# A streaming encoder layer with gathered experts: four groups of tiles instead of five, the sample's tokens on 128 partitions, the bias expanded from DRAM

## The chip, the cores and the metric

The kernel runs on one core of a Trainium2 chip. All times are device microseconds (us) of that core; lower is better. The time of a kernel is the median of its runs. One execution was profiled, and all rows of the trace are of that one.

## The reference

One layer for 1024 prompt tokens and 64 sample tokens (which have a cache of 512 keys and a running state), model width 1024, all in 32-bit floats:

```
xn = rmsnorm(x);  z = xn @ w_in                        # 1024 x 5632: q k v | f i q g | gate_a gate_b
o_a = softmax(q k' / 8 + bias[clipped distance]) v     # 8 heads of 64, own chunk of 64 and 8 before
o_b = HGRN2 recurrence in chunks of 64                 # 4 heads, state 128 x 128, rmsnorm, swish gate
h = x + (sigmoid(gate_a) * (o_a @ w_a) + sigmoid(gate_b) * (o_b @ w_b)) @ w_out
q = rmsnorm(h) @ w_query                               # 8 heads x 2 halves of 128
s = q . sub_keys; top 16 of each half, top 16 of the 256 sums  -> idx, gate (softmax)
y = rmsnorm(h + sum over 8 heads x 16 of gate * gelu(xn . u[idx]) * v[idx])    # 16384 experts
```

Outputs are y of both, the new keys and values (512 prompt rows and the 64 of the sample) and the new states. Each token of each head fetches 16 rows of u and 16 of v, 4 KB each.

## The kernel before

**Tiles and groups.** Tokens are cut into nine tiles: 0 to 7 are 128 prompt tokens each, and the tile SAMPLE has 64. `GROUPS` (line 37) lists which tiles are mixed together and at which column of the group's activations each begins: SAMPLE and 0 (192 wide), 1 and 2, 3 and 4, 5 and 6 (256 wide each), and 7 (128 wide). All tile-order loops follow this list, so SAMPLE comes first.

**Mixing, stages A to I of a group** (`mix(g)` on each engine). A: load x to `hx`, norm, turn to `xnT`. B: q, k, v. C: attention, one step for each head and tile, on keys of up to five tiles (`keys_of`, 646); SAMPLE's are the four of the cache, turned in group 0 (627), and its own. D: gate_a and w_a. E: projections of HGRN2. F: HGRN2, tile after tile. G: gate_b and w_b. H: w_out, second norm. I: w_query and, for each tile and head, scores against the sub-keys and top-k (VectorE, 1470 to 1526). "fm" products (574) have a 128 x 128 piece of the weights stationary and the group's W columns moving; "tm" products (578) have a tile's tokens stationary and 256 columns of weights moving. `plan_projections` cuts the weights into 38 blocks of 1 MB for a group; each group loads all 38 again through `wring`, three blocks deep, on SP's queue. TensorE records two instructions for each matmul of 32-bit floats.

**Experts.** A "head" q is one expert head of one tile: 72 in all. GpSimd issues 16 indirect gathers of u rows and, two heads later, 16 of v rows (`rows_in`, 547 to 560), one row of 4 KB for each token's partition, into `ring` of R = 13 slots of 128 x 1024. A slot is free again when its reader is done: VectorE reads every u row (dot product with x, line 1549) and the even v rows (1559); TensorE reads the odd v rows through a diagonal matrix of weights (854), made by ScalarE (1170). For SAMPLE all of these work on 64 partitions. At a new tile GpSimd waits for `h_out`, loads `xt` and `acc` (538 to 545), and waits for each head's top-k (`tk_done`, 553).

**Order of the work.** `interleave` (120) writes the order out for every engine alike: first the mixing of group 0 alone up to its first top-k (the start-up); then the expert heads of group g as units, with the slices of the rest of group g's top-k and of `mix(g + 1)` up to its first top-k spread between them by the estimated costs of `slices`. In the last group, where only top-k slices are left, a factor of 2.5 packs them into the first 40% of the units.

**Start-up.** SP's queue (412 to 430) loads small vectors, `rel` (the bias values in reverse), the sub-keys and the state, then x; writes `rel_scr` (427) from 8 partitions, every partition's line of 767 values repeated 128 times, shifted by one, 640 values each; then `sk_scr` (430), the turned sub-keys; then loads weights (436). ScalarE begins stage B only when `sk_scr` has landed (928). Bias tiles are loaded from `rel_scr` for each head (475) while attention runs, and VectorE adds them (1297). Engines wait for each other between stages by `enter` and `leave`.

## Time and profile before

| what | value |
|---|---|
| median of 3 runs | 4497.34 us (4483.53 to 4503.79) |
| the profiled execution's own time | 4459.93 us |
| its span, first to last instruction | 4458.2 us |
| TensorE clock granted, mean of the span | 0.806 of 2.4 GHz |
| moved by DMA | 1408.39 MB, 316 GB/s |
| gathers | 1152 of u rows, 1152 of v rows |
| loads of weight blocks | 190 of 1024 KB |

The span is what the trace covers; the time of the execution is 1.7 us longer, and the median of the runs is 37.4 us above it. PE is TensorE's matmuls, PEld its weight loads, DVE VectorE, ACT ScalarE, POOL GpSimd, SP the queue of loads and stores.

### The profile page before, as it was taken

What the parts mean: (1) busy time and instruction counts of PE and PEld (TensorE: products, weight loads), DVE (VectorE), ACT (ScalarE), POOL (GpSimd) and SP (SyncE); (2) the same over time, 40 slices, a digit from 0 to 9 for tenths busy, and PEclk for the clock granted to TensorE, in tenths of its full rate; (3) what the DMA queues carried; (4) which work ended last, traced back from release to release, by engine and by line L of the source; (5) the groups of instructions that cost most, each with busy time, mean ns of one, the idle gap of its engine ahead of it and who ended that gap; (6) DMA issues with size and microseconds to landing.
All of it is one profiled execution on the core that took longest, in us unless ns stands there. A gap on an engine that the chain in (4) does not pass through costs nothing. (4 is left out here: it accounts for less than half of the span.)

```text
span 4458.2 us, 36425 instructions
## 1 busy us (share of the span) xinstructions
PE 3141.0 (70%) x11064; PEld 1982.6 (44%) x11064; DVE 3094.0 (69%) x6491; ACT 843.8 (19%) x2079; POOL 2651.6 (59%) x2349
## 2 busy tenths in 40 slices
PE   3968558997777468876875588868765667666556
PEld 3847314464454235653652265636532345343212
DVE  0142996648849986579579956595699764858975
ACT  1221112222111123122111222211111121111101
POOL 0000566647747676568456766585577765766776
PEclk9778658598898678987987698988887788788777
DMA  5415758999999899999999999999999999999999
GB/s 130 128 59 168 179 158 198 236 287 343 355 345 356 318 340 343 396 348 346 355 346 333 332 330 385 358 349 364 334 393 346 372 374 380 359 384 372 369 404 363
DMA packets 531664, 1408.39 MB, mean 316 GB/s; under 512 B 47952, under 2 KB 223568, under 8 KB 530704
## 3 DMA queue, kind: packets, MB, share of 16 engines
q0 software_dynamic: 317856, 1149.91, 71.4%
q1 hardware_dynamic: 211088, 246.98, 17.2%
q10 hardware_dynamic: 2528, 9.18, 0.6%
q8 instruction: 91, 1.49, 0.1%
q14 instruction: 101, 0.83, 0.1%
HBM read 1385.98 MB, written 19.92 MB: 315 GB/s over the span
## 5 line engine op out<-in xcount | busy, mean ns | idle before, releaser
L854 PE MATMUL PS<-ring,diag 128*128 128x512 f32 (+1 forms) x2304 | 1481.5, 783 | 828.9 <-DMA ring<-in_peer_v,idx 590.0
L558 POOL DMA_INDIRECT ring<-in_peer_u,idx x1152 | 1347.0, 1169 | 730.1 <-issue 313.2
L558 POOL DMA_INDIRECT ring<-in_peer_v,idx x1152 | 1286.4, 1117 | 632.5 <-DVE hid L1549 316.0
L1549 DVE CUSTOM_DVE_ANT_0 ring<-ring,xt 128x1024 f32<-128x1024 f32 (+1 forms) x1152 | 1396.7, 1220 | 357.3 <-DMA ring<-in_peer_u,idx 218.5
L854 PEld LDWEIGHTS PS<-ring,diag 128*128 128x128 f32 (+1 forms) x2304 | 488.1, 230 | 1541.2 <-issue 1197.7
L574 PE MATMUL PS<-xnT,wring 128*128 128x256 f32 (+2 forms) x3840 | 781.4, 365 | 164.8 <-DMA wring<-in_w_in 94.8
L574 PEld LDWEIGHTS PS<-xnT,wring 128*128 128x128 f32 x3840 | 695.7, 204 | 287.7 <-issue 156.8
L1559 DVE SCALAR_TENSOR_TENSOR acc<-ring,wk,acc 128x1024 f32<-128x1024 f32 (+1 forms) x576 | 739.5, 1284 | 62.0 <-DMA ring<-in_peer_v,idx 49.0
L544 POOL DMA_DIRECT2D xt<-xn_scr x9 | 5.4, 602 | 423.9 <-DMA xn_scr<-arena 423.9
L1170 ACT ACTIVATE diag<-ident,wk 128x128 f32<-128x128 f32 (+1 forms) x576 | 203.3, 387 | 229.1 <-PE PS L854 135.4
L578 PE MATMUL PS<-wring,xnT 128*128 128x256 f32 (+1 forms) x864 | 201.7, 392 | 21.9 <-DMA wring<-in_w_in 21.8
L578 PEld LDWEIGHTS PS<-wring,xnT 128*128 128x128 f32 (+1 forms) x864 | 162.7, 190 | 66.3 <-DMA wring<-in_w_in 27.2
L1297 DVE SCALAR_TENSOR_TENSOR arena<-PS,bias 128x640 f32<-128x640 f32 (+3 forms) x72 | 47.9, 665 | 190.3 <-DMA bias<-rel_scr 90.3
L578 PE MATMUL PS<-wring,arena 128*128 128x256 f32 (+1 forms) x576 | 143.4, 410 | 41.1 <-DVE arena L1445 34.3
L578 PEld LDWEIGHTS PS<-wring,arena 128*128 128x128 f32 (+1 forms) x576 | 114.7, 201 | 74.4 <-issue 49.3
L574 PE MATMUL PS<-arena,wring 128*128 128x256 f32 (+2 forms) x640 | 126.5, 352 | 3.9 <-DMA wring<-in_w_branch_b 2.5
L1141 ACT ACTIVATE arena<-PS 128x256 f32<-128x256 f32 (+1 forms) x72 | 27.6, 383 | 521.5 <-PE PS L822 353.1
L574 PEld LDWEIGHTS PS<-arena,wring 128*128 128x128 f32 x640 | 110.1, 192 | 27.2 <-issue 11.3
L1242 DVE TENSOR_TENSOR arena<-PS,arena 128x256 f32<-128x256 f32 (+2 forms) x40 | 15.3, 383 | 147.0 <-PE PS L574 146.9
L1155 ACT ACTIVATE arena<-arena 128x16 f32<-128x16 f32 (+1 forms) x72 | 22.2, 308 | 495.8 <-DVE arena L1506 495.5
L662 PEld LDWEIGHTS PS<-kT,arena 64*128 64x128 f32 (+1 forms) x560 | 83.3, 214 | 44.4 <-issue 35.6
L662 PE MATMUL PS<-kT,arena 64*128 64x128 f32 (+2 forms) x560 | 99.2, 328 | 3.9 <-ACT mark_a L865 2.6
(170 smaller groups left out, 2686.6 us busy)
## 6 DMA issues: line engine op xcount, KB each, us to landing
wring<-in_w_in SPq DMA_DIRECT2D x110, 1024.0 KB, 16.4
wring<-in_peer_query SPq DMA_DIRECT2D x40, 1024.0 KB, 11.7
wring<-in_w_out SPq DMA_DIRECT2D x20, 1024.0 KB, 10.3
ring<-in_peer_u,idx POOLq DMA_INDIRECT x1152, 7.1
ring<-in_peer_v,idx POOLq DMA_INDIRECT x1152, 7.0
bias<-rel_scr SPq DMA_DIRECT2D x80, 144.0 KB, 6.1
wring<-in_w_branch_a SPq DMA_DIRECT2D x10, 1024.0 KB, 23.8
wring<-in_w_branch_b SPq DMA_DIRECT2D x10, 1024.0 KB, 14.7
```

Of the source, the lines that this page charges most:

```text
L558: pool.indirect_dma_start(ring[0:tile_rows[tn], n % R, :], None, u_tab if kind == "u" else v_tab, bass.IndirectOffsetOnAxis(ap=idx[0:tile_ ...
L574: mm = pe.matmul(PS[:, n % 2, 0:W], w[:, k, s * P:(s + 1) * P], act_in[:, k, 0:W], start=(k == 0), stop=(k == nk - 1))
L578: mm = pe.matmul(PS[0:rows, n % 2, 0:ncol], act_in[:, k, c0:c0 + rows], w[:, k, :], start=(k == 0), stop=(k == nk - 1))
L662: mm = pe.matmul(PS[0:rows, bank + n // 4, (n % 4) * P:(n % 4) * P + nk], q, kk[p0:p0 + 64, h // 2, 0:nk], start=True, stop=True)
L854: mm = pe.matmul(PS[0:rows, 6 + half, :], diag[0:rows, seq % ND, 0:rows], ring[0:rows, n % R, 512 * half:512 * (half + 1)], start=(h == 0 ...
L1141: act.activation(s1[0:rows, o % 2], PS[0:rows, 2 + o % 2, 0:2 * P] .rearrange("p (a b) -> p a b", a=2), ACT.Copy).then_inc(tk_cp, 1)
L1155: act.activation(ge[0:rows, :], cv[0:rows, :], ACT.Exp, bias=ncv[0:rows, :], accum_out=gsum[0:rows, :]).then_inc(tk_exp, 1)
L1170: act.activation(diag[0:rows, seq % ND, 0:rows], ident[0:rows, 0:rows], ACT.Copy, scale=wk[0:rows, q % 2, k:k + 1]).then_inc(diag_made, 1)
L1242: dve.tensor_tensor(M[:, c, 0:W], PS[:, n % 2, 0:W], sg[:, c, 0:W], ALU.mult)\
L1297: dve.scalar_tensor_tensor(out=sc[0:rows, i % 2, 0:w], in0=flat[0:rows, 0:w], scalar=SCALE, in1=bias[0:rows, bh % 2, off:off + w], op0=ALU ...
L1549: dve.tensor_tensor_reduce(row, row, xt[0:rows, s, :], 1.0, 0.0, ALU.mult, ALU.add, hid[0:rows, m % 2, k:k + 1]).then_inc(dve_used, 1)
L1559: dve.scalar_tensor_tensor(out=acc[0:rows, s, :], in0=ring[0:rows, n % R, :], scalar=wk[0:rows, q % 2, k:k + 1], in1=acc[0:rows, s, :], op ...
```

## The change

The groups become (0, 1), (2, 3), (4, 5) and (SAMPLE, 6, 7); the last is 320 wide. SAMPLE therefore comes after tile 5, and its cache, state and copy of the keys move to places in the arena that are free in that group (`SG`). For the experts and the top-k SAMPLE has 4 heads instead of 8, on 128 partitions: partitions 0 to 63 hold the tokens for head h, 64 to 127 the same tokens for head h + 4. Scores of both go to one bank; `xt` is loaded to both halves, `acc` is cleared in the upper one, diagonals become `sel` (two identities side by side), and at the tile's end two matmuls fold the upper half of `acc` into the sum. So there are 68 heads and 2176 gathers, all of 128 partitions. The w_query blocks of that group come in the order 0, 4, 1, 5 and so on. `rel` goes to `rel_line` in DRAM, and from there one DRAM to DRAM transfer on SP's queue makes `rel_scr`. The small loads, the sub-keys and `sk_scr` are issued by ScalarE. `bias` and `gain_hgrn` move into the arena and are filled anew in every group: padding in stage A, bias heads 0 and 1 behind x, the gain in stage C. The ring has 12 slots.

```
```diff
-GROUPS = [[(SAMPLE, 64, 0), (0, 128, 64)], [(1, 128, 0), (2, 128, 128)], [(3, 128, 0), (4, 128, 128)],
-          [(5, 128, 0), (6, 128, 128)], [(7, 128, 0)]]
+GROUPS = [[(0, 128, 0), (1, 128, 128)], [(2, 128, 0), (3, 128, 128)], [(4, 128, 0), (5, 128, 128)],
+          [(SAMPLE, 64, 0), (6, 128, 64), (7, 128, 192)]]
 NG = len(GROUPS)
 NT = sum(len(g) for g in GROUPS)
-HEADS = NT * PH
-WG = 256
+WG = 320
+MOST = max(len(g) for g in GROUPS)
+SG = [g for g in range(NG) if any(t[0] == SAMPLE for t in GROUPS[g])][0]
...
-R = 13
+R = 12
...
+def heads_in(tid):
+
+    return PH // 2 if tid == SAMPLE else PH
+
+
+TILES = [t for g in GROUPS for t in g]
+HEAD = [(tn, h) for tn, t in enumerate(TILES) for h in range(heads_in(t[0]))]
+FIRST = [HEAD.index((tn, 0)) for tn in range(NT)]
+HEADS = len(HEAD)
...
+        half = heads_in(GROUPS[g][0][0])
+        for i in range(half):
+            for h in range(i, PH, half):
+                add(g, "I", "w_query", 8, 256 * h, 256, "fm", "query")
...
+        kC = cut(arena[:, 0:2048], CB, 4 * P)
+        vC = cut(arena[:, 12 * WG:12 * WG + 2048], 4, DA)
+        kS = cut(arena[:, 12 * WG + 2048:12 * WG + 2304], CB, DEC)
+        vS = arena[:, 2048:2560]
...
+        bias = part(6144, 2, WIN)
+        gain_hgrn = part(5120, DA)
...
-                sp.dma_start(rel[:, 383:767], bass.AP(rel_bias.tensor, NREL - 1, [[NREL, HA], [-1, 384]]))\
-                  .then_inc(rel_in, 16)
...
-            sp.wait_ge(relE, 1)
-            lines = rel[:, 0:767]
-            sp.dma_start(rel_scr, bass.AP(lines.tensor, lines.offset + 127, [list(lines.ap[0]), [-1, P], [1, WIN]]))\
-              .then_inc(rel_out, 16)
-            sp.wait_ge(sk_cp, 4)
-            sp.dma_start(sk_scr, skTs.rearrange("p a b -> p (a b)")).then_inc(sk_out, 16)
...
+            def load_bias(g, h):
+                bh = g * HA + h
+                if bh >= 2:
+                    q = att_no[((bh - 2) // HA, (bh - 2) % HA, len(GROUPS[(bh - 2) // HA]) - 1)]
+                    sp.wait_ge(at_biased, q + 1)
+                for t0, j0 in ((0, 0), (64, 64)):
+                    sp.dma_start(bias[t0:t0 + 64, bh % 2, j0:j0 + 576],
+                                 rel_scr[h, t0:t0 + 64, j0:j0 + 576])\
+                      .then_inc(bias_in[bh % 2], 16)
...
+                    for h in range(2):
+                        load_bias(g, h)
+                else:
+                    sp.wait_ge(rel_mid, 16)
+                    sp.dma_start(rel_scr, bass.AP(rel_line.tensor, 127, [[768, HA], [-1, P], [1, WIN]]))\
+                      .then_inc(rel_out, 16)
+                if g == SG:
+                    enter(sp, g, "B")
+                    sp.dma_start(kc, cache_k[0, 0].rearrange("(t p) h d -> p t (h d)", p=P)).then_inc(kc_in, 16)
+                    sp.dma_start(vC, cache_v[0, 0].rearrange("(t p) h d -> p t (h d)", p=P)).then_inc(vc_in, 16)
+                    sp.dma_start(S_tile[:, :, s_slot, :], state_in[0, 0].rearrange("h k v -> k h v"))\
+                      .then_inc(state_loaded, 16)
                 load_stage(g, "B", others)
                 if g == 0:
-                    enter(sp, g, "B")
-                    sp.dma_start(kc, cache_k[0, 0].rearrange("(t p) h d -> p t (h d)", p=P)).then_inc(kc_in, 16)
-                    sp.dma_start(v[:, CACHE:CACHE + 4, :], cache_v[0, 0].rearrange("(t p) h d -> p t (h d)", p=P))\
...
+                sp.dma_start(gain_hgrn, bass.AP(hgrn_norm.tensor, 0, [[0, P], [1, DA]])).then_inc(gh_in, 16)
+                for h in range(2, HA):
+                    load_bias(g, h)
...
+                if tid == SAMPLE:
+                    pool.dma_start(xt[DEC:P, tn % 2, :], xn_scr[tid * P:tid * P + rows, :]).then_inc(xt_in[tn % 2], 16)
+                    pool.memset(acc[DEC:P, tn % 2, :], 0.0).then_inc(acc_clear, 1)
...
-                    ring[0:tile_rows[tn], n % R, :], None, u_tab if kind == "u" else v_tab,
-                    bass.IndirectOffsetOnAxis(ap=idx[0:tile_rows[tn], at:at + 1], axis=0)).then_inc(row_in[n % R], 16)
+                    ring[:, n % R, :], None, u_tab if kind == "u" else v_tab,
+                    bass.IndirectOffsetOnAxis(ap=idx[:, at:at + 1], axis=0)).then_inc(row_in[n % R], 16)
...
+                    for r0, hh in ((0, h), (DEC, h + PH // 2)) if tid == SAMPLE else ((0, h),):
+                        for p in range(2):
+                            mm = pe.matmul(PS[r0:r0 + rows, 2 + o % 2, p * P:(p + 1) * P], qp[:, 2 * hh + p, c0:c0 + rows],
+                                           skT[:, (p * PH + hh) * P:(p * PH + hh + 1) * P], start=True, stop=True)
                     mm.then_inc(tk_sc, 1)
...
+                if kind == "S" and m == stn:
+                    q = FIRST[m] + heads_in(SAMPLE) - 1
+                    pe.wait_ge(dve_used, taken["v", q, max(set(range(TOPK)) - ON_PE)][2] + 1)
+                    for half in range(2):
+                        mm = pe.matmul(PS[0:DEC, 6 + half, :], ident[:, DEC:P], acc[:, m % 2, 512 * half:512 * (half + 1)],
+                                       start=False, stop=True, skip_group_check=True)
+                    mm.then_inc(folded, 1)
...
+                                   stop=(last_head(q) and k == max(ON_PE) and tn != stn), skip_group_check=True)
...
+            with nc.allow_non_contiguous_dma(reason="small vectors laid over partitions"):
+                act.dma_start(rel[:, 383:767], bass.AP(rel_bias.tensor, NREL - 1, [[NREL, HA], [-1, 384]]))\
+                   .then_inc(rel_in, 16)
+                act.dma_start(gain_mix[:, :], norm_mix[0].rearrange("(k p) -> p k", p=P)).then_inc(const_in, 16)
+                act.dma_start(lbl[:, :, :], lb_logits.rearrange("a (h p) -> p a h", p=P)).then_inc(const_in, 16)
+            act.dma_start(sk, sub_keys[0].rearrange("a h k d -> k (a h) d")).then_inc(sk_in, 16)
+            act.wait_ge(relE, 1)
+            act.dma_start(rel_line[:, 0:767], rel[:, 0:767]).then_inc(rel_mid, 16)
+            act.wait_ge(consts, 21)
             act.wait_ge(lb_d, 1)
             act.activation(lb[:, :], lbl[:, 0, :], ACT.Sigmoid).then_inc(lb_a, 1)
             for b in range(4):
                 act.wait_ge(sk_tr, b + 1)
                 act.activation(skTs[:, 4 * b:4 * b + 4, :], PS[:, b, :].rearrange("p (a b) -> p a b", a=4), ACT.Copy)\
                    .then_inc(sk_cp, 1)
+            act.wait_ge(sk_cp, 4)
+            act.dma_start(sk_scr, skTs.rearrange("p a b -> p (a b)")).then_inc(sk_out, 16)
             leave()
 
             def norm_squares(g):
...
+                if g == SG:
+                    dve.wait_ge(kv_out, 32 * sum(len(k_tiles[q]) for q in range(g + 1)))
```

## Rows read from the trace of the kernel before

**Rows 1.** The page: the span, the engines, then GB/s in 40 slices of the span.

```profile
span 4458.2 us, 36425 instructions
PE 3141.0 (70%) x11064; PEld 1982.6 (44%) x11064; DVE 3094.0 (69%) x6491; ACT 843.8 (19%) x2079; POOL 2651.6 (59%) x2349
...
GB/s 130 128 59 168 179 158 198 236 287 343 355 345 356 318 340 343 396 348 346 355 346 333 332 330 385 358 349 364 334 393 346 372 374 380 359 384 372 369 404 363
```

**Rows 2.** Timeline of GpSimd at a border: start, us, what [idle before <-releaser].

```profile
1348.26 0.98 POOL L558 DMA_INDIRECT ring<-in_peer_u,idx  x1 [25.02 <-DVE gates L1523]
```

**Rows 3.** Windows: us, PE, PEld, DVE, ACT, POOL busy, clock, DMA share, GB/s.

```profile
441.60:1348.30 906.70, 689.25 (x2180) 414.88 (x2179) 656.27 (x1414) 168.98 (x430) 550.04 (x485) 0.75 0.87 261
1348.30:2266.40 918.10, 673.93 (x2405) 438.82 (x2405) 689.27 (x1437) 188.17 (x451) 596.84 (x516) 0.84 0.95 350
2266.40:3187.10 920.70, 674.03 (x2450) 440.69 (x2449) 690.79 (x1437) 190.64 (x452) 598.66 (x516) 0.84 0.95 350
3187.10:4045.30 858.20, 560.93 (x1960) 335.52 (x1959) 646.87 (x1363) 155.86 (x373) 590.19 (x517) 0.80 1.00 372
4045.30:4458.20 412.90, 237.97 (x503) 94.01 (x502) 316.80 (x608) 51.48 (x135) 306.89 (x288) 0.78 0.98 377
```

**Rows 4.** The last stretch: two windows, and GpSimd's waits in the second.

```profile
4045.30:4232.20 186.90, 107.72 (x304) 50.63 (x304) 168.28 (x414) 30.36 (x78) 147.86 (x129) 0.77 0.98 369
4232.20:4358.00 125.80, 67.15 (x96) 22.18 (x94) 91.15 (x125) 9.29 (x27) 96.53 (x96) 0.78 1.02 404
...
POOL ring L558 <- PE PS L854: 0.6, 2, 0.3
```

**Rows 5.** Windows: sample heads; top-k; stages D and E; G to I.

```profile
497.30:672.80 175.50, 101.47 (x164) 34.33 (x164) 171.74 (x505) 23.22 (x69) 107.77 (x97) 0.52 0.55 152
1394.00:1609.30 215.30, 113.29 (x240) 53.29 (x240) 210.85 (x610) 33.79 (x90) 148.39 (x128) 0.72 0.92 337
1883.90:1957.40 73.50, 69.39 (x280) 53.08 (x279) 38.25 (x65) 16.69 (x35) 37.73 (x33) 0.98 0.98 355
2106.10:2266.40 160.30, 136.60 (x521) 102.06 (x520) 82.20 (x158) 25.93 (x57) 72.61 (x66) 0.91 0.93 339
```

**Rows 6.** Start-up, waits and ScalarE's timeline at its first projection.

```profile
PE PS L574 <- DMA wring<-in_w_in: 45.8, 1, 45.8
...
78.03 0.33 ACT L933 ACTIVATE arena<-PS 128x192 f32<-128x192 f32 x1 [49.16 <-PE PS L574]
```

**Rows 7.** TensorE, groups of instructions by line and shape, whole span.

```profile
L574 PE MATMUL PS<-xnT,wring 128*128 128x256 f32 x2304 | 530.1, 389 | 48.2 <-ACT arena L1136 25.8 <-DMA wring<-in_w_in 16.1 <-ACT mark_a L865 6.2
L574 PE MATMUL PS<-xnT,wring 128*128 128x192 f32 x768 | 146.0, 357 | 76.1 <-DMA wring<-in_w_in 45.8 <-ACT arena L1136 28.9 <-ACT mark_a L865 0.8
L574 PE MATMUL PS<-xnT,wring 128*128 128x128 f32 x768 | 105.4, 301 | 40.5 <-DMA wring<-in_w_in 32.9 <-ACT arena L1136 6.8 <-ACT arena L1015 0.8
```

**Rows 8.** Windows of the start-up: stage C, F of the sample, F of tile 0.

```profile
114.00:173.00 59.00, 49.19 (x248) 39.59 (x248) 17.73 (x49) 22.33 (x78) 0.00 (x0) 0.53 0.32 99
256.00:291.00 35.00, 16.74 (x88) 11.56 (x88) 18.13 (x45) 7.96 (x23) 0.00 (x0) 0.53 0.14 41
291.00:340.00 49.00, 22.42 (x105) 17.49 (x105) 27.65 (x44) 9.79 (x22) 0.00 (x0) 0.60 0.12 41
```

**Rows 9.** Window in which the expansion of the bias moves alone.

```profile
44.00:60.00 16.00, 0.00 (x0) 0.00 (x0) 0.00 (x0) 0.00 (x0) 0.00 (x0) 1.00 0.46 50
```

**Rows 10.** VectorE, groups of instructions of the experts' lines, whole span.

```profile
L1549 DVE CUSTOM_DVE_ANT_0 ring<-ring,xt 128x1024 f32<-128x1024 f32 (+1 forms) x1152 | 1396.7, 1220 | 357.3 <-DMA ring<-in_peer_u,idx 218.5 <-ACT mark_a L865 72.1 <-DMA arena<-in_x_prompt 65.3
L1559 DVE SCALAR_TENSOR_TENSOR acc<-ring,wk,acc 128x1024 f32<-128x1024 f32 (+1 forms) x576 | 739.5, 1284 | 62.0 <-DMA ring<-in_peer_v,idx 49.0 <-issue 10.4
L1549 DVE DVE_READ_ACCUMULATOR2_ANT hid<- 128x1 f32 (+1 forms) x1152 | 92.7, 80 | 0.0
```

**Rows 11.** What GpSimd waited for, whole span: us, times, longest.

```profile
POOL ring L558 <- DVE hid L1549: 335.9, 132, 22.0
POOL ring L558 <- PE PS L854: 298.3, 124, 13.7
```

260 lines of the change are left out of this document (127 added, 133 removed).

## The prediction, made before the changed kernel ran

> **What bounds the kernel now.** I began with the page: no engine is full (TensorE 70% busy, VectorE 69%, GpSimd 59%), and of the forty slices those behind the start-up move 158 to 287 GB/s, the later ones 313 to 404 [rows 1]. So the mean shares say little, and the next view was the table of windows, cut where the experts of a new group begin: the first gather behind a long wait for the gates of its top-k [rows 2]. Six stretches come out, the first up to 441.6 us [rows 3]: a start-up of 441.6 us without a gather, three stretches of 907, 918 and 921 us in which 16 expert heads run beside the mixing work of the next group of two tiles, one of 858 us beside the one-tile group, and a last one of 413 us with 8 heads and no mixing. A full head costs 32 gathers. Where nothing else runs, three heads take 125.8 us (41.9 each) at 404 GB/s, and GpSimd waits 0.6 us of them for a free slot [rows 4]. That is the floor of a head. In the mixing stretches a head costs 57 us on average, because three kinds of zone are bound elsewhere [rows 5]: the top-k zone by VectorE (210.9 of 215.3 us busy), the projections of stages D and E by TensorE (69.4 of 73.5 us), stages G and H with a chain of norms (136.6 of 160.3 us). The sample's heads stand out: their gathers fetch rows for 64 partitions only, yet three of them take 175.5 us at 152 GB/s with VectorE at 98%. A half-filled head is not half as dear; it is as dear as a full one.
>
> **The change, stretch by stretch.** The sum is made against the span of 4458.2 us; the profiled execution's own time is 4459.9 us, 37.4 us below the median of 4497.3, so the end adds 1.7 and 37.4.
>
> **Start-up: 441.6 to 419 us.** Now the first projection waits: TensorE stands from 27 to 73 us for the first block of w_in, with ScalarE behind it [rows 6], because that load sits on SP's queue behind the expansion of the bias, and ScalarE's stage B also wants sk_scr written. After the change the first three blocks go out on SP right behind x, and the small loads, the sub-keys and sk_scr sit on ACT's queue. ScalarE's own chain reaches stage B at about 29 us (it stands idle for 49.2 us before its first copy at 78.0 [rows 6]); I take 31 for the first product, 42 us earlier. The group is 256 wide instead of 192: a matmul of a feature-major product leaves two records, of 530.1/2304 = 0.230 us at 256 and 146.0/768 = 0.190 at 192 [rows 7]; up to the first top-k there are about 350 such matmuls, 350 x 2 x 0.04 = 28, say 30 us. Attention has 1 + 2 key tiles a head instead of 5 + 1; stage C took 59 us and half its matmuls go, but the step-to-step chain stays: -22 (between -10 and -30). Stage F has a full tile (49 us) in place of the sample's (35 us) [rows 8]: +14. The four turns of the cache: -3. Sum -42 + 30 - 22 + 14 - 3 = -23, between -40 and -5.
>
> The expansion itself (8 x 128 rows of 2560 B) is the edit whose price the trace does not show. Now it moves at 50 GB/s with the DMA share at 0.46, alone in that window [rows 9], so 2.62 MB take about 52 us on about half the engines. From DRAM the nearest row is the gathers' 404 GB/s [rows 4], half of which on half the engines would be 13 us. It starts at about 14 us (rel_line must land first), so it lands between 27 and 66. The fourth block of w_in queues behind it and is wanted at 31 + 3 x 7 = 52 (a block is 16 matmuls of 0.46 us). I take 25 us, landing at 39, hidden; the upper end costs 15 us. Bias heads 0 and 1 now arrive before stage C; VectorE's wait for them was nearly all behind the late first block and is not counted again.
>
> The Trainium skill (DMA: Bandwidth & Descriptors, section on why a DMA increments its semaphore by 16) says that a DMA uses the largest number of engines up to 16 that divides the size of its slowest dimension. Here that is 8 heads, before and after, so by that rule moving the source to DRAM does not spread it over 16 engines; the measured share of 0.46 agrees, and it is why I do not count 16 engines. With 16 it would land at about 30 us, and the sum would be the same.
>
> **Groups 0 and 1: 907 + 918 to 915 + 918.** Group 0 becomes 16 full heads beside two full tiles, which is what 918 us stands for; two key tiles fewer in attention take some 3 us off. The half-filled heads go, but full ones come in their place, so nothing is won here.
>
> **Group 2: 921 to 1011.** Its mixing partner is now three tiles, 320 wide. From one tile to two TensorE's busy time rose from 560.9 to 674.0 us, by 113, and the time by 62.5 [rows 3]. The third tile brings: feature-major products, 448 matmuls x 2 records x 0.046 (64 columns by the slope of 0.73 ns between 128 and 256, [rows 7]) = 41; token-major ones, 80 matmuls x 2 x 0.235 = 38; attention, 40 key tiles at the 49.19/48 = 1.02 us of the start-up's stage C [rows 8], where the clock was 0.53, so at 0.84 I take 0.87: 35; stage F and transposes 25 (22.4 us in one full tile of the start-up, [rows 8]): 139 us. At the same ratio (62.5/113 = 0.55) that is 77 us of time; if all of it shows, 139. The zones where it falls are the ones already at 94% TensorE [rows 5], and the same fifteen top-k must share 3.96 heads instead of 4.8, so I take 90.
>
> **Groups 3 and 4: 858 + 413 = 1271 to 949.** One stretch of 20 heads (4 + 8 + 8), nothing mixed. The two-head lag of v makes 21 heads' worth. Nineteen top-k are spread over the first 8 heads, 2.4 each. Four such heads with seven top-k took 186.9 us with VectorE 168.3 busy [rows 4]; a head's own VectorE work is 16 x 1.30 + 8 x 1.28 = 31.1 us [rows 10], so a top-k costs (168.3 - 124.4)/7 = 6.3 us and 2.4 of them make 46 us at 98% busy: 48 a head. 8 x 48 + 13 x 41.9 = 929. The stretch of today, 412.9, less 186.9 and five heads of 41.9, leaves a tail of 16.5; 3 for the folding matmuls and the sample's extra load: 949. Here is the gain: 16 expert heads no longer share their time with a fifth pass over 38 weight blocks of 1 MB, and four heads' worth of gathers (128 of 2304) are gone from the kernel.
>
> **Ring of 12.** GpSimd waits for a free slot 335.9 us on line 1549 and 298.3 on line 854, 256 times [rows 11]. Where VectorE or TensorE sets the pace a slot less costs nothing; where it only bridges a jolt, it costs a gather of 1.3 us each. Ends 0 and 60; I take 10.
>
> **Edits at nothing.** Three DMAs and one clear for the sample's tile on GpSimd's queue come once, in a boundary where it waits 25 us for gates anyway, as at every border [rows 2]; without that cover, 4 us. gain_hgrn (256 KB) and the padding of the bias once a group: under 2 us against a DMA queue with slack in stage C. SP's new wait in the last group (enter B before the cache loads) come where blocks 0 to 2 already landed and the fourth waits for product 0 in any case. The sample's v lies in M's place, so M waits in stage D until the k and v outputs have landed: a whole attention stage later.
>
> Sum: 4458.2 - 23 + 8 + 0 + 90 - 322 + 10 = 4221 of span; plus 1.7 and 37.4: **4260 us**. The bytes allow it: 38 MB of weights and some 4 MB more are gone, which alone is 104 to 120 us at 404 to 350 GB/s.
>
> **Rivals.** (a) *The wide group pays in full.* If the third tile costs 139 and every jolt of the ring shows (60), the time is 4260 + 49 + 50 = 4360; for it speaks that TensorE would be 80% busy over that stretch, against it that one to two tiles cost only 0.55 of theirs. 4330 to 4440, chance 0.17. (b) *The expansion stays slow*: it keeps 52 us in DRAM too, the fourth block comes 15 us late: 4275. It lies inside the forecast's own range and has 0.2 of it. (c) *More is won*: the third tile at 60 us or less, as the second was, start-up at 400: 4260 - 30 - 19 = 4211; without the ring's 10 and with the far end of stage C's gain, 4193. Chance of below 4200: 0.10. (d) *The ring decides.* If 13 slots are what limits the gathers everywhere, every us behind the start-up grows by 13/12: 3804/12 = 317 us more, 4577, slower than before. It decides from the point where GpSimd waits for slots in the zone without mixing; there it waits 0.6 us of 125.8 for one [rows 4, 11], against which stand the 634 us elsewhere. Chance 0.06. (e) *Only the start-up and the empty heads pay*, the rest going back into the dense zones: around 4490, chance 0.03.
>
> **Numbers.** Forecast (4200 to 4330) 0.64. The range 4175 to 4365 takes in the third tile between 50 and 139, the start-up's ends, the ring up to 50 and the shift between a profiled execution and a median. A measurement of this kernel tells about 0.5% (22 us) from no change. Faster by more than that: 0.64 + 0.17 + 0.10 = 0.91; same: 0.03; slower: 0.06.
>
> **What would show it.** Stretches near 419, 915, 918, 1011 and 949 us; first product near 31 us; 2176 gathers; a DMA share of about 0.5 under the expansion; the third stretch with TensorE near 813 us busy. I am wrong if a stretch of 16 heads beside two tiles moves by over 20 us (the ring), if the third is over 1060 us, or if the last one's heads without top-k cost over 44 us.

## The result: 2.4% faster, less than half of what was forecast

| | before | after |
|---|---|---|
| median of the runs | 4497.3 us (4500.2 with a fourth run, which the ratio takes in) | 4393.4 us (4379.8 to 4395.9) |
| ratio, 95% interval | | 0.9764 (0.9732 to 0.9796) |
| profiled execution, span | 4459.9, 4458.2 us | 4379.8, 4378.0 us |

The forecast was 4260 us with a range of 4175 to 4365. The sign was right, the size was not: 104 us were won, not 237, and the result lies above the range.

The page of the changed kernel, against [rows 1]: the span, the engines, GB/s in the 40 slices, and the DMA totals.

```profile
span 4378.0 us, 33505 instructions
...
PE 3049.8 (70%) x10044; PEld 1858.3 (42%) x10044; DVE 2952.0 (67%) x6145; ACT 789.5 (18%) x1946; POOL 2555.3 (58%) x2221
...
GB/s 132 148 19 168 294 314 334 356 391 333 346 358 348 326 332 320 374 360 348 365 321 330 289 276 314 333 288 284 338 287 264 345 317 345 347 366 383 383 368 333
DMA packets 491091, 1365.49 MB, mean 312 GB/s; under 512 B 45081, under 2 KB 185881, under 8 KB 490273
```

The bytes fell by 42.9 MB, as the forecast had them ("38 MB of weights and some 4 MB more"). The half-filled heads' slices of 158 to 287 GB/s right behind the start-up are gone. A new low appears between slices 21 and 31, at 264 to 338 GB/s: the stretch beside the group of three tiles. The windows show it. They are cut as in [rows 3] (us, busy PE, PEld, DVE, ACT, POOL with instructions, granted clock, DMA share, GB/s): start-up, heads 0 to 15, 16 to 31, 32 to 47, 48 to 67.

```profile
0.00:442.20 442.20, 329.95 (x1450) 280.69 (x1451) 103.01 (x243) 89.18 (x226) 8.63 (x27) 0.83 0.37 117
442.20:1338.60 896.40, 645.18 (x2261) 426.96 (x2260) 662.41 (x1416) 177.12 (x430) 561.20 (x485) 0.82 0.94 339
1338.60:2270.00 931.40, 692.05 (x2449) 450.42 (x2449) 690.95 (x1439) 190.31 (x452) 594.07 (x517) 0.82 0.94 346
2270.00:3361.60 1091.60, 818.93 (x3003) 509.31 (x3003) 726.41 (x1509) 219.69 (x543) 633.53 (x518) 0.83 0.85 300
3361.60:4378.00 1016.40, 563.64 (x886) 190.91 (x884) 769.21 (x1542) 113.22 (x296) 757.89 (x676) 0.72 0.94 354
```

| stretch | forecast | measured | miss |
|---|---|---|---|
| start-up | 419 | 442.2 | +23 |
| heads 0 to 15 | 915 | 896.4 | -19 |
| heads 16 to 31 | 918 | 931.4 | +13 |
| heads 32 to 47, beside three tiles | 1011 | 1091.6 | +81 |
| heads 48 to 67 | 949 | 1016.4 | +67 |
| ring of 12 (forecast apart from the stretches; what it costs is inside them) | 10 | - | -10 |
| from the span to the median | 39 | 15.4 | -24 |

That sums to +131 of the 133 us (the rest is rounding). Two stretches carry the miss.

GpSimd's waits in the changed kernel (us, times, longest), which answer to [rows 11]: over the whole span the waits for a slot stay what they were, 319.9 and 312.0 us where they were 335.9 and 298.3.

```profile
POOL ring L590 <- DVE hid L1609: 319.9, 122, 15.4
POOL ring L590 <- PE PS L898: 312.0, 87, 19.9
POOL ring L590 <- DVE gates L1584: 86.0, 6, 41.1
...
POOL xt L573 <- DMA out<-acc: 16.5, 1, 16.5
```

In the third stretch alone they are 261.0 us (the rows below), where the same stretch of before had 89.9 and 66.0, together 155.9. So 105 of its 171 us more are waits of GpSimd for TensorE and VectorE to free a slot.

```profile
POOL ring L590 <- PE PS L898: 134.7, 34, 13.0
POOL ring L590 <- DVE hid L1609: 126.3, 49, 13.0
```

### The profile page after: what moved, and what is told of

It is laid out like the page before. It is cut to its first block and busy times, and to the rows that moved or that the text cites. A ratio compares the mean times of both kernels' runs of the same rounds, so it can differ in the third digit from the quotient of the medians.

```text
span 4378.0 us, 33505 instructions
## 1 busy us (share of the span) xinstructions
PE 3049.8 (70%) x10044; PEld 1858.3 (42%) x10044; DVE 2952.0 (67%) x6145; ACT 789.5 (18%) x1946; POOL 2555.3 (58%) x2221
## 2 busy tenths in 40 slices
DMA packets 491091, 1365.49 MB, mean 312 GB/s; under 512 B 45081, under 2 KB 185881, under 8 KB 490273
## 5 line engine op out<-in xcount | busy, mean ns | idle before, releaser
L898 PE MATMUL PS<-ring,diag 128*128 128x512 f32 (+1 forms) x2176 | 1437.1, 800 | 932.1 <-DMA ring<-in_peer_v,idx 697.1
L590 POOL DMA_INDIRECT ring<-in_peer_v,idx x1088 | 1297.7, 1193 | 675.1 <-issue 326.8
L590 POOL DMA_INDIRECT ring<-in_peer_u,idx x1088 | 1238.4, 1138 | 695.2 <-DVE hid L1609 311.0
L1609 DVE CUSTOM_DVE_ANT_0 ring<-ring,xt 128x1024 f32<-128x1024 f32 x1088 | 1322.0, 1221 | 406.6 <-DMA ring<-in_peer_u,idx 260.1
L898 PEld LDWEIGHTS PS<-ring,diag 128*128 128x128 f32 (+1 forms) x2176 | 479.9, 240 | 1660.3 <-issue 1439.6
L606 PE MATMUL PS<-xnT,wring 128*128 128x256 f32 (+1 forms) x3072 | 753.0, 406 | 80.6 <-ACT arena L1191 52.6
L1621 DVE SCALAR_TENSOR_TENSOR acc<-ring,wk,acc 128x1024 f32<-128x1024 f32 x544 | 699.2, 1285 | 55.6 <-DMA ring<-in_peer_v,idx 39.1
L606 PEld LDWEIGHTS PS<-xnT,wring 128*128 128x128 f32 x3072 | 604.2, 198 | 242.1 <-issue 87.8
L573 POOL DMA_DIRECT2D xt<-xn_scr x9 | 5.5, 606 | 434.7 <-DMA xn_scr<-arena 418.1
L1224 ACT ACTIVATE diag<-masks,wk 128x128 f32<-128x128 f32 x512 | 185.7, 396 | 395.4 <-PE PS L898 170.6
L1354 DVE SCALAR_TENSOR_TENSOR arena<-PS,arena 128x640 f32<-128x640 f32 (+3 forms) x72 | 47.9, 665 | 147.3 <-PE PS L694 92.8
L606 PE MATMUL PS<-arena,wring 128*128 128x256 f32 (+1 forms) x512 | 122.5, 392 | 0.0
L694 PE MATMUL PS<-kT,arena 64*128 64x128 f32 x480 | 88.6, 336 | 47.1 <-issue 24.3
L694 PEld LDWEIGHTS PS<-kT,arena 64*128 64x128 f32 x480 | 74.0, 231 | 72.9 <-issue 44.3
## 6 DMA issues: line engine op xcount, KB each, us to landing
arena<-in_x_prompt SPq DMA_DIRECT2D x16, 512.0 KB, 10.2
```

The source lines that it names most:

```text
L590: pool.indirect_dma_start(ring[:, n % R, :], None, u_tab if kind == "u" else v_tab, bass.IndirectOffsetOnAxis(ap=idx[:, at:at + 1], axis=0 ...
L606: mm = pe.matmul(PS[:, n % 2, 0:W], w[:, k, s * P:(s + 1) * P], act_in[:, k, 0:W], start=(k == 0), stop=(k == nk - 1))
L694: mm = pe.matmul(PS[0:rows, bank + n // 4, (n % 4) * P:(n % 4) * P + nk], q, kk[p0:p0 + 64, h // 2, 0:nk], start=True, stop=True)
L898: mm = pe.matmul(PS[0:rows, 6 + half, :], diag[:, seq % ND, 0:rows], ring[:, n % R, 512 * half:512 * (half + 1)], start=(h == 0 and k == m ...
L1224: act.activation(diag[:, seq % ND, 0:rows], sel[:, :] if rows == DEC else ident, ACT.Copy, scale=wk[:, q % 2, k:k + 1]).then_inc(diag_made, 1)
L1354: dve.scalar_tensor_tensor(out=sc[0:rows, i % 2, 0:w], in0=flat[0:rows, 0:w], scalar=SCALE, in1=bias[0:rows, bh % 2, off:off + w], op0=ALU ...
```

## The experiments

Each was made from the kernel before or from the changed kernel ("after"). Stretches are named as above. The two theories at the start: **T1**, the wide group costs more than forecast and eats what the saved pass brings; **T2**, the ring of 12 slots slows every head.

### The ring, in both kernels

```
b_r12, b_r11 (from before):   -R = 13     +R = 12 / R = 11
a_r11 (from after):           -R = 12     +R = 11
```

> The kernel before with a ring of 12 slots instead of 13, nothing else. Theory A (a slot bridges jolts only): the two stretches beside two tiles grow by the 13 us that the changed kernel's second stretch shows over its likeness before (931 against 918), the last stretch's heads without top-k stay near 42 us, in all 20 to 50 us slower than before (ratio 1.004 to 1.011). Theory B (the ring makes the 4 us a head that the changed kernel's last stretch lost, 45.9 against 41.9): those heads cost 45 to 46 here too. Theory C (the ring limits everywhere): 13/12 of all behind the start-up, over 300 us slower.

> The kernel before with 11 slots. With 12 slots its last stretch's heads without top-k or mixing rose from about 42 to 45.4 us (profile of each). If depth did that, 11 slots give 47 to 50. If it is that with an even number of slots a slot always takes u rows or always v rows, 11 gives 42 again. If it is neither but the spread between executions, 44 to 46, as in the changed kernel with 12 and with 11.

> The changed kernel with 11 slots instead of 12. Theory A: one more slot costs somewhat more than the first, 30 to 60 us in all (ratio to the kernel before 0.985 to 0.99). Theory B: the heads without mixing and top-k rise from 45.9 to about 50 us. If the ring is nothing, within 10 us of the changed kernel (4393).

Before with 12 slots: 4514.3 us against 4501.7, ratio 1.0033 (1.0011 to 1.0054). Before with 11: 4519.2 in a single run, against 4505.1. After with 11: 4393.6 us, the same as with 12. So the slot costs 13 to 15 us in before, where I had put 10, and with 11 slots no further cost shows; the 20 to 50 us and the 30 to 60 us of theory A were too much. It sits in the dense stretches: the first three with gathers take 920, 926 and 935 us with 12 slots against 907, 921 and 922 with 13 (profiles of b_r12 and b_again). The heads without mixing and top-k take 45.4 us with 12 slots and 45.1 with 11; b_again below shows 44.5 with 13. T2 and rival (d), 317 us, fall.

### The sample's heads: 64 partitions again

```
 def heads_in(tid):
-    return PH // 2 if tid == SAMPLE else PH
+    return PH
...
-                    ring[:, n % R, :], None, u_tab if kind == "u" else v_tab,
+                    ring[0:tile_rows[tn], n % R, :], None, u_tab if kind == "u" else v_tab,
```

> The changed kernel with the sample's tile as 8 expert heads on 64 partitions again (72 heads, 2304 gathers, no folding), in its new place in the last group. If an empty half costs what a full one does, four more heads at 46 to 50 us, and four more top-k of 6 us in part hidden: 180 to 220 us slower than the changed kernel, which is slower than before by about 80 us (ratio 1.015 to 1.025). If half-filled heads run at half price where no mixing is in the way: under 60 us slower than the changed kernel.

Without the fold the changed kernel takes 4545.0 us, ratio 1.0101 to before (1.0060 to 1.0143): slower than before by 1%. The fold is worth 4545.0 - 4393.4 = 152 us (180 to 220 were expected), and **everything else in the change together costs about 43** (4545.0 against 4501.7). Its last stretch, in the same columns as above, has 24 heads instead of 20:

```profile
3342.00:4534.60 1192.60, 717.79 (x1082) 235.00 (x1080) 916.41 (x1850) 133.19 (x353) 889.67 (x804) 0.67 0.90 303
```

That is 1192.6 - 1016.4 = 176 us for four heads more (and their four top-k), 44 each, the price of a full head: a head of 64 rows costs what one of 128 costs, as [rows 5] had it.

The whole kernel gains less, mostly because the fold also costs something, which my text had overlooked. The first top-k of the folded tile needs the queries of two heads, 0 and 4, before a gather can start. The third stretch without the fold, and GpSimd's first gather behind it:

```profile
2266.80:3342.00 1075.20, 800.33 (x2932) 497.79 (x2931) 726.39 (x1509) 216.77 (x539) 635.68 (x516) 0.84 0.86 303
...
3342.02 0.93 POOL L587 DMA_INDIRECT ring<-in_peer_u,idx  x1 [24.25 <-DVE gates L1576]
```

With the fold that gather waits 41.1 us for its gates and the stretch takes 1091.6 us. So 16 us of the third stretch belong to the fold and not to the third tile.

### The five groups of before, with the rest of the change

```
-GROUPS = [[(0, 128, 0), (1, 128, 128)], [(2, 128, 0), (3, 128, 128)], [(4, 128, 0), (5, 128, 128)],
-          [(SAMPLE, 64, 0), (6, 128, 64), (7, 128, 192)]]
+GROUPS = [[(SAMPLE, 64, 0), (0, 128, 64)], [(1, 128, 0), (2, 128, 128)], [(3, 128, 0), (4, 128, 128)],
+          [(5, 128, 0), (6, 128, 128)], [(7, 128, 0)]]
...
-        kt_before = {g: sum(len(k_tiles[q]) for q in range(g)) for g in range(NG + 1)}
+        kt_before = {g: sum(len(k_tiles[q]) for q in range(g)) + (4 if g > SG else 0) for g in range(NG + 1)}
```

> The changed kernel with the five groups of before (SAMPLE and 0; 1, 2; 3, 4; 5, 6; 7), all else as changed: the sample folded on 128 partitions, ring of 12, the new start-up. Theory A (the fold is the gain, the regrouping a loss of some 45 us): 4320 to 4360, faster than the changed kernel by 30 to 70 us. My prediction's theory (the fifth pass over the weights costs 60 us and more, and goes with the regrouping): slower than the changed kernel, 4420 or more.

4322.9 us, ratio 0.9592 (0.9563 to 0.9622): 70 us **below** the changed kernel. The windows of its start-up, of its first stretch (now 12 heads), of the 16 heads beside the one-tile group, and of the last eight heads:

```profile
0.00:415.40 415.40, 314.95 (x1647) 268.76 (x1647) 93.72 (x239) 90.31 (x243) 10.00 (x30) 0.83 0.43 134
415.40:1162.10 746.70, 528.82 (x1983) 352.60 (x1983) 513.20 (x1108) 145.83 (x369) 423.19 (x356) 0.82 0.89 314
...
3031.20:3889.70 858.50, 556.49 (x1971) 336.08 (x1970) 647.57 (x1365) 155.09 (x373) 596.78 (x517) 0.80 1.00 372
3889.70:4320.70 431.00, 240.64 (x492) 93.45 (x490) 316.50 (x608) 51.70 (x135) 321.52 (x288) 0.77 0.96 361
```

The first stretch goes from 906.7 to 746.7 us [rows 3]: the fold's 160 us, all in one place. The start-up goes from 441.6 to 415.4, by 26 us: the edits to the loads bring 33 up to the first product (73.0 to 40.3), and the folded tile's first pair of heads takes 9.5 back in stage I. The first group of the changed kernel, 256 wide and with two full tiles, needs 27 us more than this one (442.2). And the 16 heads beside one tile run at a DMA share of 1.00, in 858.5 us as before the change: that the transfers bind them is worked out by stages below.

### The three tiles first instead of last

```
-GROUPS = [[(0, 128, 0), (1, 128, 128)], [(2, 128, 0), (3, 128, 128)], [(4, 128, 0), (5, 128, 128)],
-          [(SAMPLE, 64, 0), (6, 128, 64), (7, 128, 192)]]
+GROUPS = [[(SAMPLE, 64, 0), (0, 128, 64), (1, 128, 192)], [(2, 128, 0), (3, 128, 128)],
+          [(4, 128, 0), (5, 128, 128)], [(6, 128, 0), (7, 128, 128)]]
...
-        kt_before = {g: sum(len(k_tiles[q]) for q in range(g)) for g in range(NG + 1)}
+        kt_before = {g: sum(len(k_tiles[q]) for q in range(g)) + (4 if g > SG else 0) for g in range(NG + 1)}
```

> The changed kernel with the three-tile group first (SAMPLE, 0, 1; then 2, 3; 4, 5; 6, 7): the third tile's mixing runs in the start-up, beside no expert. Theory A (in the third stretch nothing hid the third tile): it costs about the same there as beside 16 heads, the start-up grows by 150 to 180 us from 442, the third stretch falls back to 920 to 935, and the time stays within 40 us of the changed kernel. If experts and mixing overlapped in part, the start-up grows by more than the third stretch falls, and the time rises by over 60 us.

4363.6 us in a single run, within 40 us of the changed kernel as theory A has it, and the stretches beside two tiles fall back to 943.9 and 927.6 us. Windows: start-up, the 20 heads of the first group, 16 heads beside tiles 4 and 5, 16 heads beside the last group, the last 16 heads.

```profile
0.00:622.10 622.10, 481.30 (x2009) 356.94 (x2010) 137.91 (x313) 124.01 (x323) 10.01 (x29) 0.82 0.30 93
622.10:1682.70 1060.60, 725.44 (x2355) 430.72 (x2355) 814.29 (x1729) 198.58 (x484) 713.23 (x615) 0.80 0.95 350
1682.70:2626.60 943.90, 692.19 (x2448) 451.81 (x2447) 690.95 (x1439) 190.07 (x452) 592.59 (x517) 0.83 0.93 342
2626.60:3554.20 927.60, 686.61 (x2449) 449.30 (x2449) 691.50 (x1439) 189.83 (x452) 596.86 (x516) 0.83 0.95 348
3554.20:4361.70 807.50, 459.50 (x789) 178.34 (x787) 617.12 (x1229) 92.95 (x242) 594.37 (x546) 0.75 0.96 362
```

Here the third tile is mixed with no expert head beside it, and costs 622.1 - 442.2 = 180 us. In the changed kernel it is mixed beside 16 heads and costs 1091.6 - 920.7 = 171 us [rows 3]. Both figures hold the fold's first pair of heads. Beside the heads it was hidden almost not at all. Two tiles take 442 us alone, 42 of it before the first product, and add 190 to 200 to 16 heads without any mixing or top-k (16 x 45.5 = 728 us), so these hide a little over 200; of the third tile's 180 they hide 9. That settles T1 for this kernel: the third tile shows nearly in full.

### What in the third tile costs it

Both leave out work in the steps of heads 32 to 47 alone. In a_halfv half of what TensorE adds up of the v rows (columns 512 to 1023) is left out; in a_halfu the dot products with the u rows cover columns 0 to 511 only.

```
a_halfv:
-                for half in range(2):
+                for half in range(1 if 32 <= m < 48 and not (h == 0 and k == min(ON_PE))
+                                  and not (last_head(q) and k == max(ON_PE)) else 2):
a_halfu:
+                        row, xr = (row[:, 0:512], xt[:, s, 0:512]) if 32 <= m < 48 else (row, xt[:, s, :])
```

> The changed kernel with TensorE's share of the experts' work halved in the third stretch alone: in the units of heads 32 to 47 the second half (columns 512 to 1023) of each v row on TensorE is left out. That takes some 75 us off TensorE's 819 us in that stretch and leaves the gathers as they are. If TensorE bounds the mixing of three tiles, the stretch of 1092 us falls by 55 to 75 us. If chains between the engines or VectorE bound it, it falls by under 25 us.

> The changed kernel with VectorE's work on the u rows halved in the third stretch alone: the dot products of heads 32 to 47 run over columns 0 to 511. That takes some 150 us off VectorE's 726 us there. If TensorE bounds the stages D, E, G, H, I and VectorE only top-k and F, the top-k zone's four heads (about 60 us each) fall to the floor of 42 to 46 and the stretch by 60 to 90 us; if VectorE is nowhere the bound, under 25 us.

The third stretch of each (first a_halfv, then a_halfu; us, PE, PEld, DVE and on):

```profile
2268.30:3339.10 1070.80, 740.51 (x2756) 485.60 (x2754) 726.36 (x1509) 219.55 (x543) 643.24 (x519) 0.76 0.87 306
```

```profile
2276.60:3327.20 1050.60, 802.70 (x3004) 501.31 (x3003) 591.35 (x1509) 218.78 (x543) 564.00 (x519) 0.86 0.87 312
```

78 us less on TensorE bring 21, a ratio of 0.27 (with a granted clock of 0.76 where it was 0.83); 135 us less on VectorE bring 41, a ratio of 0.30, between the two answers expected. Neither engine is the bound over the whole stretch. By stages the two runs part cleanly. The stretch is cut here at TensorE's first matmul of each stage; "rest of top-k" is what comes ahead of the mixing, and stage I is counted up to the next stretch (us):

| stage | before, two tiles | changed, three tiles | more time | more TensorE busy | a_halfv | a_halfu |
|---|---|---|---|---|---|---|
| rest of top-k | 286.1 | 269.0 | -17 | -18 | 268.5 | 246.9 |
| A (turns), B | 61.2 | 81.8 | +21 | +17 | 79.0 | 83.0 |
| C, attention | 139.6 | 172.5 | +33 | +32 | 170.2 | 166.7 |
| D | 51.7 | 62.0 | +10 | +10 | 58.4 | 62.0 |
| E | 66.3 | 91.2 | +25 | +25 | 84.3 | 91.2 |
| F, HGRN2 | 159.0 | 219.9 | +61 | +34 | 220.4 | 205.9 |
| G | 57.8 | 61.7 | +4 | +7 | 59.9 | 63.3 |
| H | 57.1 | 73.8 | +17 | +19 | 70.5 | 71.1 |
| I | 41.9 | 59.7 | +18 | +19 | 59.6 | 60.5 |

Outside F the time grows by what TensorE's busy time grows by (110 and 111 us). In D and E TensorE is busy without a gap; work taken off it shortens them (by 3.6 and 6.9 us), work taken off VectorE does not. In the top-k and in F it is the other way round: a_halfu takes off 22 and 14 us, a_halfv nothing.

### The start-up: what ScalarE issues

Two theories for a first product at 42.0 us instead of 31: the sub-keys land late (they are issued fourth on ScalarE's queue), or ScalarE stands at the issue of the small vectors. ScalarE's timeline in the changed kernel (start, us, what):

```profile
0.80 0.62 ACTq L912 DMA_DIRECT2D arena<-in_rel_bias  x1
1.45 16.18 ACTq L914 DMA_DIRECT2D gain_mix<-in_norm_mix  x1
17.66 1.94 ACTq L915 DMA_DIRECT2D lbl<-in_lb_logits  x1
19.83 0.88 ACTq L916 DMA_DIRECT2D arena<-in_peer_subkeys  x1
```

```
a_sk1:  act.dma_start(sk, sub_keys...) moved ahead of rel_bias, gain_mix and lb_logits
a_sp:   rel_bias, gain_mix and lb_logits moved to the head of SP's queue, ahead of x
```

> The changed kernel, with ScalarE issuing the sub-keys ahead of the small vectors (4 bytes an element, which held its queue for 16 us and let the sub-keys land at 26.3 us). If that order was why the first product came at 42.0 us instead of 31: first product at 31 to 35 us, the start-up 7 to 11 us shorter (432 to 435), the time 0.2% lower. If the 3 MB of weights on SP's queue were the cause, the sub-keys still land behind 20 us and the start-up gains under 4 us.

> The changed kernel with the three small vectors back on SP's queue, ahead of x and the weights; sub-keys, rel_line and sk_scr stay with ScalarE. If ScalarE stood 16 us in issuing 4-byte transfers because 3 MB of weights held the same engines, the first product comes at 29 to 33 us instead of 42.0 and the first gather at 430 to 433 instead of 442.2. If the start-up is bound by something behind it (the expansion, the fourth block of w_in), stage B grows by what is won and the first gather stays above 438.

With the sub-keys first they landed at 10.9 us instead of 26.3, yet ScalarE still stood 14.2 us at gain_mix and the first product came at 40.6, the first gather at 439.1: neither of the two theories, but the hold on ScalarE; 4382.6 us, 0.9732 (0.9694 to 0.9770), not to be told from after. With the vectors on SP (a single run, 4372.7 us) the first product came at 29.2 and the first gather at 427.7 instead of 442.2. TensorE's timeline in that run:

```profile
10.72 3.64 PE L636 MATMUL PS<-masks,arena 128*128 128x128 f32 x16 [10.72 <-DMA arena<-in_peer_subkeys]
...
29.18 5.06 PE L611 MATMUL PS<-xnT,wring 128*128 128x256 f32 x11 [1.85 <-ACT mark_a L914]
```

So it was the issue: ScalarE stood 16 us at the issue of gain_mix. The expected 29 to 33 us for the first product came, and the start-up won a little more than expected.

### The jolt at head 51, and the border

```
a_best1 = a_sp, and in units():
-            if m - last < 3:
-                now.append(("F", tn, m - last, 0))
+            if m == last: now.append(("F", tn, 0, 0))
+            elif m == last + 1:
+                now.insert(0, ("F", tn, 1, 0)); now.append(("F", tn, 2, 0))
and in stage I the scores of the first key ahead of two query products
```

> The changed kernel with three edits: the small vectors on SP's queue (as in a_sp); the last two steps of a tile's output moved one head earlier (step 1 to the start of the next head, step 2 to its end), so that tile 6 finds y of tile 5 stored although only the sample's four heads lie between; and at a group's border the first key scores directly behind the w_query products that they need, before two products of the next head. Expected: head 51 falls from 66.5 to 47 to 50 us and GpSimd's wait of 16.5 us for out<-acc goes; the wait for gates at the last border falls from 41 to about 32 us and at the others from 25 to about 18; the start-up loses 10 us. In sum 45 to 55 us less than the changed kernel, near 4345 (ratio 0.964 to 0.969). If the jolt at head 51 has another cause, 25 us less.

In the changed kernel the load of xt for tile 6 waits for the store of y of tile 5, because only the sample's four heads lie between. GpSimd's timeline, and the window of that head:

```profile
3571.66 0.59 POOL L573 DMA_DIRECT2D xt<-xn_scr  x1 [16.54 <-DMA out<-acc]
```

```profile
3506.60:3573.10 66.50, 31.94 (x51) 7.86 (x49) 61.65 (x167) 12.32 (x29) 40.24 (x34) 0.71 0.77 287
```

With the output steps a head earlier that wait is gone, the head takes 49.9 us instead of 66.5 and the last stretch 997.2 instead of 1016.4. The edit at the border brought next to nothing: the first gather of the last border waits 42.0 us for its gates against 41.1, at the two others 9.9 and 9.5 against 12.1. Together 4353.3 us, 0.9646 (0.9606 to 0.9686), 40 us below the changed kernel where 45 to 55 were expected.

### Before, profiled again

No edit; the question is whether 41.9 us is the floor of a head [rows 4].

> The kernel before once more, for a second profile. If 13 slots make the last stretch's heads without mixing or top-k cost 41.9 us against 45.4 with 12 or 11, they cost 41 to 43 here and the last stretch is 410 to 418 us. If the first profile was a lucky one, they cost 44 to 46 and the last stretch is 430 or more.

4496.3 us, and its windows of the last eight heads and of the same three heads as in [rows 4]:

```profile
4056.60:4494.60 438.00, 243.02 (x494) 94.76 (x493) 317.33 (x608) 51.48 (x135) 316.07 (x288) 0.76 0.94 355
```

```profile
4251.30:4384.80 133.50, 74.14 (x96) 23.29 (x94) 91.30 (x124) 9.19 (x27) 98.30 (x97) 0.68 0.98 379
```

44.5 us a head, not 41.9. Of the 36.4 us by which this span is longer, 25.1 lie in the last stretch (438.0 against 412.9) and 11.3 in the 4056 us ahead of it. The profile that I worked from was a quick execution, and quick where gathers run alone.

### Other versions

> Five groups: 0 and 1; 2 and 3; 4 and 5; 6 and 7; the sample's tile alone, 64 wide, folded. With the small vectors on SP, the output steps one head earlier, and 13 slots (three-tile buffers are not needed). Theory A says that a stretch of 16 heads beside a small group stays at the floor of the DMA queues: start-up 429, 897, 931, 931, then about 830 for 16 heads beside the sample's mixing, and 240 for the last four heads: 4240 to 4290 in all, the best of all kernels. If a pass over 40 MB of weights costs in proportion to its bytes, the fourth stretch is 930 and the time 4350 or more.

> The five groups of before with the fold (as f_before), the small vectors back on SP's queue, and 13 slots, which fit since no group has three tiles. The start-up loses 12 to 14 us against f_before (415 to about 402), the slot gives back 15 us spread over the stretches: 4290 to 4300, ratio 0.952 to 0.956, the best of all. If 13 slots are worth nothing here, 4308 and the stretches as in f_before (934, 935, 858, 431).

g5_best has the groups (0,1), (2,3), (4,5), (6,7) and the sample alone, with both edits of a_best1 that worked and 13 slots: 4336.6 us, 0.9614 (0.9582 to 0.9646), where 4240 to 4290 was expected. Its fourth stretch, 16 heads beside the sample's group, takes 896.5 us at a DMA share of 0.97, where 830 was expected, so it does not beat f_before. That is 40 us more than 16 heads beside tile 7 alone need in f_best (857.0), with the same weights and a narrower group; no run shows why. f_best is f_before with the small vectors on SP and 13 slots: **4294.5 us, 0.9547 (0.9515 to 0.9579)**, the best of all: its start-up takes 408.2 us (some 402 were expected) and its last eight heads 433.1, as the windows show. Of the 28 us to f_before 7 are the start-up; the other 21 are left to the thirteenth slot, against 15 expected.

```profile
0.00:408.20 408.20, 319.18 (x1646) 273.04 (x1647) 93.65 (x239) 89.86 (x243) 10.01 (x29) 0.80 0.44 136
...
3858.80:4291.90 433.10, 247.88 (x496) 95.90 (x494) 316.46 (x608) 51.65 (x135) 322.07 (x288) 0.72 0.95 359
```

## Why the prediction was wrong, point by point

**The failed step: "At the same ratio (62.5/113 = 0.55) that is 77 us of time ... so I take 90."** The overlap was wrong: the third tile's work (the sample's, 64 columns) was counted as half hidden, and it shows in full. The stretch grew by 171 us (1091.6 - 920.7), 155 by the third tile and 16 by the fold's first pair of heads (a_s64). Its work was right: TensorE 818.9 us busy where 813 was named, and the records at 320 wide take 214.6/768 = 0.279 us each where the slope gave 0.276:

```profile
L606 PE MATMUL PS<-xnT,wring 128*128 128x320 f32 x768 | 214.6, 439 | 18.4 <-ACT arena L1191 8.2 <-DMA wring<-in_w_in 7.0 <-ACT mark_a L909 2.5
```

What was wrong is the ratio. It was taken from the step from one tile (858.2) to two (920.7), and the two stretches are not bound by the same thing. Stages D and E show it, in windows of before beside one tile, of before beside two, and of the changed kernel beside three:

```profile
3675.90:3798.60 122.70, 89.44 (x441) 70.16 (x442) 57.07 (x94) 23.76 (x50) 61.51 (x60) 0.87 1.02 382
2753.30:2871.30 118.00, 117.71 (x498) 94.31 (x497) 52.77 (x85) 22.63 (x47) 59.41 (x52) 1.00 0.99 362
2793.30:2946.50 153.20, 153.20 (x569) 104.09 (x570) 58.64 (x89) 24.47 (x50) 66.87 (x58) 1.00 0.83 284
```

With one tile TensorE is busy 89.4 of 122.7 us while the DMA share is 1.02, and it waits 26.4 us for blocks of w_in: the transfers set the pace. The second tile fills TensorE's gaps and costs nothing there (118.0 us). From then on TensorE is busy without a gap, and the third tile's 35.5 us of work take 35.2 us of time, while the DMA share falls to 0.83. So 62.5 us is not what a tile costs; it is what shows above a pace that the transfers set. The rows said so: the 0.55 had a DMA share of 1.00 against 0.95 beside it [rows 3], and TensorE was already at 94% in D and E with two tiles [rows 5], but I read only the totals of TensorE. A better sum, from 16 heads at 45.5 us each with nothing mixed (728 us): one tile with its top-k adds 130, two 190 to 200, three 347 (364 with the fold's pair).

My ceiling of 139 was too low as well, by one term. Against the table by stages above: the products, 79 us named, came to 78 (A, B, D, E, G, H and I are 94 us longer, 16 of them the fold's); attention, 35 named, came to 33; the rest of top-k got 17 shorter; stage F, 25 named, came to 61. I had priced F at TensorE's busy time in a full tile, 22.4 us, though that tile took 49 us [rows 8]. Before and after:

```profile
2871.30:3030.30 159.00, 100.43 (x320) 50.09 (x320) 152.99 (x232) 34.22 (x81) 125.62 (x103) 0.82 0.96 351
2946.50:3166.40 219.90, 134.34 (x429) 66.11 (x428) 189.99 (x303) 44.72 (x110) 172.70 (x127) 0.74 0.86 309
```

VectorE is busy 153.0 of 159.0 us there with two tiles and 190.0 of 219.9 with three, and a_halfu shortens it by 14 us. What the remaining gaps are, the tile passed from engine to engine or something else, no run shows by itself. Rival (a), "the wide group pays in full", had the right mechanism; that its 4330 to 4440, at a chance of 0.17, holds the result is in part luck, since 50 of its us were further jolts of the ring, where the runs show 13 to 21 us for the slot in all, and the last stretch's miss took their place.

**Heads 48 to 67: 949 forecast, 1016.4 measured.** The count was right (no top-k is missing, 20 heads, a two-head lag). The jolt at head 51 was foreseen by nothing in my text; a_best1 puts it at 19 us. The rest is the floor of a head, 41.9 taken, measured here over nine heads without top-k at 410.9/9 = 45.7:

```profile
3859.20:4270.10 410.90, 223.48 (x288) 71.69 (x287) 272.03 (x374) 32.07 (x86) 309.08 (x291) 0.71 0.98 373
```

Thirteen such heads make 49 us. Most of that is the quick profile: I added the 37.4 us between it and the median once, as a constant, while 25 of them belonged to eight heads of this kind, which the change turned into 20. Against the profile of before taken again (44.5) the heads are dearer by 1.2 each, 16 us in all, whose cause no run shows; 12 slots are not clearly it, since before with 12 has 45.4 and with 11 45.1.

**Start-up: 419 forecast, 442.2 measured.** The bottleneck was rightly named: TensorE's wait of 45.8 us for w_in [rows 6] is gone, and the first product came at 42.0 us instead of 73. But "31 for the first product" missed that ScalarE has to issue the small loads that I moved to its queue in my own text: moved DMAs have an issue time, 16.18 us for one of them, and a_sp shows them to be the whole difference (29.2). That is 11 us. Cut at TensorE's first matmul of each stage, as above, the wider group and its full tile cost some 10 more than the 30 + 14 of the sum: stages B, D, E, F, G and I are 5.8, 10.2, 5.6, 18.2, 10.5 and 4.2 us longer than before. Attention with the four turns of the cache gave 22 (62.5 to 40.2) where I had 22 + 3.

**The expansion: hidden, as forecast.** It was issued at 26.5 us, 12 later than I took, and from 40 to 200 us the waits of no engine name a DMA: neither the fourth weight block behind it nor the bias in stage C came late. From 40.0 us on it moves alone (all packets are of SP's queue), and from 45.0 to 50.9 us, when SP issues the next block, nothing moves:

```profile
40.00:44.50 4.50, 2.60 (x10) 2.10 (x10) 0.06 (x1) 1.95 (x9) 0.00 (x0) 0.87 0.52 208
45.00:50.90 5.90, 5.90 (x24) 5.01 (x24) 0.00 (x0) 0.39 (x1) 0.00 (x0) 0.85 0.00 1
```

So from DRAM it runs at 208 GB/s where it had 50, lands by 45.0 us, and by that rate its 2.62 MB take about 13 us, the lower end of my estimate, against the 25 that I took. The Trainium skill's rule (DMA: Bandwidth & Descriptors, section on why a DMA increments its semaphore by 16) would keep it on 8 engines of 16; the share of 0.52 agrees. Rival (b), "it keeps 52 us in DRAM too", was wrong in its premise.

**Groups 0 and 1: right** within 20 us (896.4 and 931.4 against 915 and 918). "Nothing is won here" for group 0 was 10 us too cautious; the 13 us more of group 1 are of the size that the slot costs in such a stretch (5 to 13 us, b_r12). **The ring: right in size** (10 taken; 13 to 15 measured in before, 21 between f_before and f_best, none between 12 and 11).

**Groups 3 and 4: the gain was there, but not where I put it.** From before's second profile the two stretches go from 862.3 + 438.0 to 1016.4, 284 us less, where 322 stood in the sum. Of it about 152 to 160 us are the fold's four heads (a_s64, f_before). The other 124 to 132 us are the saved fifth pass, and the third tile's 171 with the start-up's 27 take more than all of that back. "A fifth pass over 38 weight blocks of 1 MB" was given as the gain, and it is one; but the tile of that pass had to go somewhere, and beside two others it costs more than the pass it saved.

Taken apart from the medians: fold about -152 to -160, edits of the start-up -26, ring +15, regrouping +70 (f_before against after; 77 by their ratios, 0.9592 and 0.9764); sum -93 to -101, measured -104.

## What to carry to other kernels

A stream of fixed work hides only so much beside it: before widening a group, price the stream alone and take what each tile adds above it; here 16 heads (728 us alone) hid some 200 us of mixing and next to nothing of a third tile, so five narrow groups beat four with a wide one. A ratio between two stretches is usable only if the same thing binds both: compare the DMA column and the busy share of the fullest engine, stage by stage. Where an engine has gaps a further tile can hide in them (D and E with one tile); where it has none, every further us of its work shows. Price a stage by its time where it passes work between engines, not by the busy time of one of them. And when a change bundles several edits, ask of each alone: one (the fold) gave 3.4%, one cost 1.6%, and the version without the regrouping is the better kernel.
